# A fourth buffer for the experts' gate matrices, and expert code for twelve experts in a loop

## The reference

```python
# D_MODEL = 1024, 4 groups x 8 experts = 32, TOP_K = 2, D_EXPERT = 512
_, gsel = lax.top_k(lg, 1)                       # one of 4 groups for each token
tv, ti = lax.top_k(le_g, TOP_K)                  # two of its 8 experts
gates = jnp.sum(jax.nn.one_hot(eid, N_EXPERTS) * w[..., None], axis=1)
for e in range(N_EXPERTS):
    h = jax.nn.silu(x @ w_g[e]) * (x @ w_u[e])   # gate (1024x512) and up (1024x512)
    y = y + gates[:, e:e + 1] * (h @ w_d[e])     # down (512x1024)
return x + y                                     # then a final RMSNorm
```

## Time and profile before

| | us |
|---|---|
| three runs | 890.99, 897.95, 897.75; median 897.75 |
| profiled execution, device time | 895.14 |
| its span, first to last instruction | 892.7 |
| TensorE busy | 764.6 (86%) |
| mean share of the DMA engines' time, queue q1 | 69.6% |
| DMA traffic in all | 255.37 MB |

### The profile page before, as it was taken

One profiled execution on the slowest core, in us unless ns is written; L12 is line 12 of the kernel. 1 busy time (PEld: TensorE's weight loads), 2 busy tenths in 40 slices (PEclk: granted clock), 3 DMA queues, 4 the chain that ended last, 5 costly groups with the idle time before them and its releaser, 6 DMA issues.

```text
span 892.7 us, 15309 instructions
## 1 busy us (share of the span) xinstructions
PE 764.6 (86%) x5066; PEld 489.9 (55%) x5067; DVE 319.7 (36%) x754; ACT 214.0 (24%) x445; POOL 168.7 (19%) x380
## 2 busy tenths in 40 slices
PE   6999967799799982999979888879999999999740
PEld 3555545558454552666645454546666666666420
DVE  3578698850224334222212111112122212222117
ACT  4001235401331221122221122112222222222113
POOL 2015013200001002222222122112222222222100
PEclk9999988995889995899999899989999999999885
DMA  8202061171853349499999999999999949999965
GB/s 353 80 1 109 31 76 53 21 224 20 307 206 122 137 189 379 169 418 417 419 418 420 417 420 418 419 419 419 419 403 378 417 194 390 417 422 416 417 242 246
DMA packets 59593, 255.37 MB, mean 286 GB/s; under 512 B 19851, under 2 KB 22795, under 8 KB 36369
## 3 DMA queue, kind: packets, MB, share of 16 engines
q1 hardware_dynamic: 52560, 242.86, 69.6%
q0 software_dynamic: 6240, 11.46, 3.4%
q10 hardware_dynamic: 768, 0.72, 0.2%
HBM read 241.38 MB, written 22.30 MB: 295 GB/s over the span
## 4 chain that ended last, share of the span: by engine, by line
PE 57%; DMA 16%; SPq 13%; DVE 8%; ACT 3%; issue 2%; POOLq 0%; POOL 0%; DVEq 0%; ACTq 0%
PE pair L944 15%; PE pair L966 9%; DMA slot<-in_w_exp_up 7%; PE pair L742 7%; PE pair L605 6%; SPq L331 4%; SPq L334 4%; DMA reg_f<-in_w_exp_up 4%; SPq L325 3%; PE pair L945 3%; DMA slot<-in_w_in_qkv 2%; PE pair L847 2%; PE pair L920 2%; PE pair L606 2%; PE pair L667 2%
## 5 line engine op out<-in xcount | busy, mean ns | idle before, releaser
L944 PE MATMUL pair<-slot,probs 128*64 128x256 f32 x800 | 189.3, 398 | 22.8 <-DMA slot<-in_w_exp_up 21.7
L945 PE MATMUL pair<-slot,probs 128*64 128x256 f32 x800 | 189.5, 398 | 0.0
L944 PEld LDWEIGHTS pair<-slot,probs 128*64 128x64 f32 x800 | 114.3, 144 | 78.5 <-issue 46.3
L1590 DVE TENSOR_TENSOR sums<-iota_t,sums 128x640 bf16<-128x640 f32 x38 | 32.0, 841 | 259.0 <-POOL sums L536 252.9
L945 PEld LDWEIGHTS pair<-slot,probs 128*64 128x64 f32 x800 | 114.4, 144 | 0.0
L944 PE MATMUL pair<-reg_h,probs 128*64 128x256 f32 x384 | 88.1, 389 | 8.5 <-DMA reg_f<-in_w_exp_up 8.4
L966 PE MATMUL pair<-slot,sums 128*64 128x512 f32 x400 | 91.3, 597 | 4.5 <-ACT sums L1156 4.5
L945 PE MATMUL pair<-reg_f,probs 128*64 128x256 f32 x384 | 88.2, 389 | 0.0
L512 POOL DMA_INDIRECT probs<-hf_scr,row_u x38 | 40.1, 1056 | 240.4 <-DVE row_u L1602 183.8
L605 PE MATMUL pair<-reg_h,slot 128*128 128x512 f32 x160 | 82.4, 597 | 2.9 <-DVEq L1245 1.9
L1648 DVE TENSOR_TENSOR probs<-pair,probs 64x256 f32<-64x256 f32 x74 | 31.5, 426 | 136.9 <-ACT probs L1154 91.2
(11 more groups left out here) (365 smaller groups left out, 1033.1 us busy)
## 6 DMA issues: line engine op xcount, KB each, us to landing
slot<-in_w_exp_gate SPq DMA_DIRECT2D x22, 2048.0 KB, 22.8
slot<-in_w_exp_up SPq DMA_DIRECT2D x22, 2048.0 KB, 26.9
slot<-in_w_exp_down SPq DMA_DIRECT2D x44, 1024.0 KB, 24.0
reg_h<-in_w_exp_gate SPq DMA_DIRECT2D x10, 2048.0 KB, 23.9
reg_f<-in_w_exp_up SPq DMA_DIRECT2D x10, 2048.0 KB, 28.7
reg_h<-in_w_exp_down SPq DMA_DIRECT2D x10, 512.0 KB, 21.0
reg_f<-in_w_exp_down SPq DMA_DIRECT2D x10, 512.0 KB, 21.8
probs_t<-in_w_exp_down SPq DMA_DIRECT2D x10, 512.0 KB, 21.9
```

The source lines that it names most:

```text
L944: pe.matmul(gu[j][0:TT], lhs, gate_w[q][:, h, c, out], start=n == 0, stop=n == KD - 1)
L945: ins = pe.matmul(gu[j][TT:P], lhs, up_w[q][:, h, c, out], start=n == 0, stop=n == KD - 1)
L1590: tt(sel, iota_t[:].unsqueeze(1).to_broadcast([P, NT, P]), place_of[:, 0].unsqueeze(2).to_broadcast([P, NT, P]), ALU.is_equal)
```

## The change

Four buffers for gate matrices in place of three; the fourth is `reg_x`, columns 0 to 4095. Expert e now uses gate buffer e % 4 and, as before, up and down set e % 3. Expert 3's gate matrix is loaded ahead of the loop, behind the last load of expert 2, once the five tiles of normed rows are transposed (`xf_tr`) and stored (`hf_kept`). In the loop SyncE issues, for expert e: up(e), gate(e + 1), and after `y_ready` down(e). Gate(e + 1) goes where the gate matrix of expert e - 3 was, so it waits for the same event as up(e). The last expert has no gate matrix behind its up matrix.

Since 3 and 4 buffers come round together after twelve experts, TensorE's loop has twelve bodies and runs twice; experts 24 to 31 are written out behind it. SyncE's loop has twelve bodies from expert 3 on and runs twice, with experts 27 to 31 behind it.

```diff
@@ -202,7 +202,7 @@
 
 
         halves = lambda x: x.rearrange("p (h c n) -> p h c n", h=2, c=4)
-        gate_w = [halves(r[:, 0:4096]) for r in (slot[0], slot[1], reg_h)]
+        gate_w = [halves(r[:, 0:4096]) for r in (slot[0], slot[1], reg_h, reg_x)]
         up_w = [halves(r) for r in (slot[0][:, 4096:8192], slot[1][:, 4096:8192], reg_f[:, 0:4096])]
         down_w = [[x[:, 8192 + D * k:8192 + D * k + D] for k in range(KH)] for x in slot]
         down_w += [[reg_h[:, 4096:5120], reg_f[:, 4096:5120], probs_t[:], kv_f[:, 0:D]]]
@@ -244,10 +244,11 @@
             y_copied fin_out fin_sq fin_ms fin_sqrt fin_done sc_read base_step place_ready rows_done
             pow_ready ffn_ms ffn_sqrt fin_ss""".split()
 
-        names += [f"{n}_in{q}" for n in ("gate", "up", "down") for q in range(3)]
+        names += [f"{n}_in{q}" for n, held in (("gate", 4), ("up", 3), ("down", 3)) for q in range(held)]
         names += [f"got{i}" for i in range(NT)]
         s = {n: sem(n) for n in names}
-        gate_in, up_in, down_in = [[s[f"{n}_in{q}"] for q in range(3)] for n in ("gate", "up", "down")]
+        gate_in, up_in, down_in = [[s[f"{n}_in{q}"] for q in range(held)]
+                                   for n, held in (("gate", 4), ("up", 3), ("down", 3))]
         got_in = [s[f"got{i}"] for i in range(NT)]
 
         block = ctx.enter_context(nc.Block())
@@ -320,8 +321,10 @@
             sp.dma_start(o["state_prompt"], h_last[:]).then_inc(s["states_out"], 16)
             sp.dma_start(o["state_sample"], h_dec[:]).then_inc(s["states_out"], 16)
 
-            def load_gate_up(q, e):
-                sp.dma_start(gate_w[q], gate_v[e]).then_inc(gate_in[q], 16)
+            def load_gate(g, e):
+                sp.dma_start(gate_w[g], gate_v[e]).then_inc(gate_in[g], 16)
+
+            def load_up(q, e):
                 sp.dma_start(up_w[q], up_v[e]).then_inc(up_in[q], 16)
 
             def load_down(q, e):
@@ -335,7 +338,8 @@
 
 
             sp.wait_ge(s["y_ps"], 8)
-            load_gate_up(0, 0)
+            load_gate(0, 0)
+            load_up(0, 0)
             load_down(0, 0)
 
 
@@ -376,21 +380,28 @@
             sp.wait_ge(s["pairs_used"], 1)
             sp.dma_start(down_w[2][KH - 1], down_v[2, :, 1, 1]).then_inc(down_in[2], 16)
 
+            sp.wait_ge(s["xf_tr"], NT)
+            sp.wait_ge(s["hf_kept"], 16 * NT)
+            load_gate(3, 3)
+
             sp.wait_ge(s["pos_done"], 1)
 
-            def load_expert(q, e):
+            def load_expert(n, e, more):
 
                 done = sp.value_load(first_i[0:1, bass.ds(e - 2, 1)], min_val=1, max_val=TILES_MAX)
                 sp.wait_ge(s["gu_ready"], done)
-                load_gate_up(q, e)
+                load_up(n % 3, e)
+                if more:
+                    load_gate((n + 1) % 4, e + 1)
                 sp.wait_ge(s["y_ready"], done)
-                load_down(q, e)
-
-            with sp.Fori(1, NE // 3) as it:
-                for q in range(3):
-                    load_expert(q, it * 3 + q)
-            for e in range(NE - NE % 3, NE):
-                load_expert(e % 3, e)
+                load_down(n % 3, e)
+
+            rounds = (NE - 3) // 12
+            with sp.Fori(0, rounds) as it:
+                for n in range(12):
+                    load_expert(3 + n, it * 12 + (3 + n), True)
+            for e in range(3 + 12 * rounds, NE):
+                load_expert(e, e, e + 1 < NE)
 
             done = sp.value_load(first_i[0:1, NE - NE % 3:NE - NE % 3 + 1], min_val=1, max_val=TILES_MAX)
             sp.wait_ge(s["y_ready"], done)
@@ -929,19 +940,21 @@
             turn()
             pe.wait_ge(s["pos_done"], 1)
 
-            def expert(q, e, loads):
-
+            def expert(n, e, rounds):
+
+                g, q = n % 4, n % 3
+                gates, loads = rounds * 3 + (n // 4 + 1), rounds * 4 + (n // 3 + 1)
                 first, end = tiles_of(pe, e)
                 with pe.Fori(first, end) as w:
                     pe.wait_ge(s["xt_copied"], w + 1)
-                    pe.wait_ge(gate_in[q], loads * 16)
+                    pe.wait_ge(gate_in[g], gates * 16)
                     pe.wait_ge(up_in[q], loads * 16)
                     for j in range(2):
                         out = slice(256 * j, 256 * j + 256)
                         for n in range(KD):
                             h, c = n // 4, n % 4
                             lhs = xt_e[:, c, TT * h:TT * h + TT]
-                            pe.matmul(gu[j][0:TT], lhs, gate_w[q][:, h, c, out], start=n == 0, stop=n == KD - 1)
+                            pe.matmul(gu[j][0:TT], lhs, gate_w[g][:, h, c, out], start=n == 0, stop=n == KD - 1)
                             ins = pe.matmul(gu[j][TT:P], lhs, up_w[q][:, h, c, out], start=n == 0, stop=n == KD - 1)
                         ins.then_inc(s["gu_half" if j == 0 else "gu_ready"], 1)
 
@@ -968,11 +981,11 @@
                                             start=k == 0, stop=k == KH - 1)
                     ins.then_inc(s["y_ready"], 1)
 
-            with pe.Fori(0, NE // 3) as it:
-                for q in range(3):
-                    expert(q, it * 3 + q, it + 1)
-            for e in range(NE - NE % 3, NE):
-                expert(e % 3, e, NE // 3 + 1)
+            with pe.Fori(0, NE // 12) as it:
+                for n in range(12):
+                    expert(n, it * 12 + n, it)
+            for e in range(NE - NE % 12, NE):
+                expert(e % 12, e, NE // 12)
 
 
         @block.scalar
```

## The result

The changed kernel takes **890.45 us** (median of 20 runs, 887.96 to 897.61), the kernel before 897.13 (20 runs on the same chip); the ratio is 0.9943 with a 95% interval of 0.9926 to 0.9960. In three later sessions it was 0.9966 (0.9941 to 0.9990), 0.9936 (0.9910 to 0.9962) and 0.9933 (0.9899 to 0.9968). The forecast was 889.0. The profiled execution took 890.42 us with a span of 888.2.

What follows compares the result with a forecast made beforehand. Bound taken as the experts' weight stream, with TensorE the bound from 607 to 736 us. On the 892.7 us span: -9.0 + 2.0 = -7.0, so 885.7; as device time 888.1 or 890.7, given as 889.0; range 881.5 to 900.0.

Steps and rivals of the forecast that it cites:

- the case: Whole kernel: 9.0 us gained from the weight stream less 2.0 us for code, 885 to 891.5 us; chance 0.50.
- That rival: Ahead of the experts: expert 3's gate matrix delays the first gather by up to 5.4 us, 890 to 894; chance 0.10.
- the one of the unused buffer: Expert loop: SyncE comes too late for the fourth buffer, only the order changes, 895 to 898 us; chance 0.05.
- First stretch: Up to expert 17: up matrix lands 5.4 us earlier, down matrix does not, so 3.4 us gained.
- Last stretch: Restart to expert 31's up matrix: 19 matrices instead of 20 at 5.50 us each, 5.5 us gained.
- the prediction's meeting at expert 30: Expert 30's down product: TensorE free at 831.8 us, its down matrix there at 831.9.
- the term that was mis-sized: Code packets of the twelve-body loop: one more on the slowest DMA engine in each weight-bound stretch, +2.0 us.
- The slower rival: Weight-bound stretches: all code packets on one DMA engine, net +3 to +8 us, 898 to 905; chance 0.15.
- The jump back: TensorE between experts 11 and 12: a short stall is hidden in the 4.0 us an expert leaves free.
- the Trainium skill's rule: TensorE's loop: a taken branch outside the 2-page window forces a fetch; the prediction doubted this, given 128 KiB or 2048 instructions.
- No idle piece of 2 us or less should bring: Waits inside tiles ahead of down products: too short to bring half clock, 0.66 us a matmul in place of 0.40.
- The dent: Late in the expert loop: the dip in DMA activity becomes 6 us wide in place of 9.

Runs made afterwards that it cites:

- e12: The kernel before, unchanged, profiled and timed once more: ratio 0.9996.
- e1: The kernel before with only the twelve-body loops on TensorE and SyncE, three gate buffers and the old load order: ratio 1.0011.
- e2: The changed kernel with gate(e + 1) issued behind down(e) instead of ahead of it: ratio 0.9946.
- e6: The kernel before, old order, six bodies ahead of a three-body loop, fourth buffer for the gate matrices of experts 3 and 31 only: ratio 0.9972.
- e9: e10 plus four unused products ahead of TensorE's wait for expert 17 and four ahead of that for expert 30: 888.64 us, ratio 0.9895.
- e10: e6 with experts 15 to 17 written out, without unused products: 891.66 us, ratio 0.9938.
- e5: e2 with five unused products ahead of TensorE's wait for expert 31: ratio 0.9984.
- e11: The changed kernel as it is, run again against the kernel before: ratio 0.9933.
- e8: The changed kernel as it is, run again in another session against the kernel before: ratio 0.9936.
- e4: The kernel before with TensorE's loop at six bodies and two experts behind it, SyncE as before: ratio 0.9982.
- e7: e6 with the fourth buffer used for expert 3 alone, every later gate matrix loaded as before: ratio 0.9962.

## Why the prediction was right, and where it was off

**Direction and size.** Forecast 7.0 us on the profiled span, which became 4.5 us shorter; the expert part gave 4.4, and the timed median 6.7. The range and the case (a smaller stream, part of the gain given to code and to waits inside the tile) were right.

**Expert 3's gate matrix ahead of the loop.** Issued at 347.04 (forecast 346). It holds nothing up: the first gather takes 6.65 us (6.5 to 6.8 in the four profiles), for 7.18 in the earlier trace rows and 6.15 in e12. That rival fell, and so did the one of the unused buffer, since SyncE issues gate(e + 1) 0.6 us behind up(e).

**First stretch.** The mechanism was right: up(17) early, down(17) not, so the down product waits for the down matrix, at 614.42 (forecast 612.5 to 614). The gain is 1.5 us by the means of the table, in place of 3.4. Up(17) lands 3.4 us earlier for a forecast of 5.4. e1 attributes most of the difference to code: down(17) lands 1.1 to 1.5 us later by the code alone, and 0.1 to 0.5 us more in the changed kernel, which stay open. e2 shows the waiting itself to be the order's doing.

**Last stretch.** From restart to up(31) it takes 106.6 to 106.9 us, 3.5 less than before; forecast 5.5. e6, e9 and e10, without the twelve bodies, measure 105.0 to 105.2, so one matrix less is worth 5.1 and the changed kernel gives 1.4 to 1.9 of it back. e1 has 1.3 of code there; the rest may lie in the order of the loads, in which e6, e9 and e10 differ too. Nor did the prediction's meeting at expert 30 hold: it had TensorE free for that down product at 831.8 us and the matrix there at 831.9, without a wait. TensorE was free at 833.5, as late as the first stretch had made it, and the matrix landed at 835.7, 101.0 us behind the restart in place of 99.0:

```profile
835.89 6.42 PE L979 MATMUL pair<-slot,sums 128*64 128x512 f32 x16 [2.36 <-DMA slot<-in_w_exp_down]
```

**The code: the term that was mis-sized.** 39 packets came, within the 35 to 45 forecast, and I put 2.0 us on the sum for them. e1 gives 2.5 us, and it is up to 3.0 with the 1.4 to 1.9 of the last stretch in place of e1's 1.3. The count was right; one more on the slowest engine in each stretch, at 1.0 us, was too little. On which engines the packets fell no view shows. The slower rival, all packets on one engine, would have made the kernel 3 to 8 us slower and is excluded. The jump back cost a gap of 3.3 us without a releaser (in all four profiles; 5.0 and 4.9 in e2 and e5), inside the slack of the first stretch as the prediction had it: expert 17's tile is governed by the landing of its down matrix alone. On the Trainium skill's rule in "Runtime: NRT & Kernel Launch", section on instruction fetch mechanics: the packets disagree with its 2-page window (six bodies are jumped back over with no new load) and are compatible with its 2048 instructions for TensorE, which lie between six bodies and twelve: a tile shows 207 instructions of TensorE in the trace (its weight loads, waits and branches with it), and some 230 as I count them in the program.

**"No idle piece of 2 us or less should bring" the slow clock: this step failed.** Expert 30's down product, shown above, follows a wait of 2.36 us in a tile that had no wait ahead of it, and takes 6.42 us; in the first stretch of the same profile waits of 1.8 to 2.5 us are followed by down products of 5.1 to 5.4 us in six tiles, and waits of 1.7 to 2.3 us by products of 3.65 in three. Of its timeline two rows, and the stretches of these two products (the granted clock stands third from the end):

```profile
485.42 5.35 PE L979 MATMUL pair<-slot,sums 128*64 128x512 f32 x16 [2.10 <-DMA slot<-in_w_exp_down]
...
501.32 3.65 PE L979 MATMUL pair<-slot,sums 128*64 128x512 f32 x16 [1.68 <-DMA slot<-in_w_exp_down]
...
485.40:490.80 5.40, 5.35 (x16) 1.78 (x16) 0.00 (x0) 0.00 (x0) 0.39 (x3) 0.68 1.01 413
501.30:505.00 3.70, 3.65 (x16) 1.26 (x16) 0.00 (x0) 0.00 (x0) 0.81 (x4) 1.00 0.98 409
```

In e11 it came behind a still shorter one:

```profile
581.58 5.31 PE L979 MATMUL pair<-slot,sums 128*64 128x512 f32 x16 [1.20 <-DMA slot<-in_w_exp_down]
```

So it is not the wait's length alone that decides: after 2.52 us e8 ran expert 30's at full clock. The 1.5 to 1.7 us of each slow product of the first stretch lie in slack, and so do the 2.8 at expert 30 but for 0.5. So the false step cost the forecast little. On the other side, taking the long waits ahead of the tiles away, which is where the prediction saw a gain at expert 30 alone, was worth more than it said: where such a wait comes back at the end of a stretch (tile 17 in e2, e4, e6, e7, e10), 2.6 to 3.0 us are lost.

**The dent.** Forecast 6 us wide in place of 9, from the last landing at 727.0 to a restart 3.4 us earlier. The last landing ahead of it is that of the second half of down(24), at 704.27 + 24.8 = 729.07:

```profile
704.27 0.35 SPq L334 DMA_DIRECT2D slot<-in_w_exp_down  x1
...
slot<-in_w_exp_down SPq DMA_DIRECT2D x1, 1024.0 KB, 24.8
```

The next load is issued at 734.67, so the dent is 5.6 us wide (5.5 to 5.6 in the four profiles, 9.1 and 9.2 in the two of before). The width was forecast rightly, but for other dates, and that is luck: in the count of the table the restart came 1.5 us earlier and not 3.4, and the last landing 2.2 us later and not at the same time. The DMA engines do not run dry together; over the last 9.7 us ahead of the restart their share is already down to 0.19.

**The sum of the miss** in the expert part: forecast 7.0, that is 9.0 less 2.0 for code; measured 4.4. The first stretch gave 1.5 for its term of 3.4 (1.9 less), the last one 3.5 for 5.5 up to the landing of up(31) (2.0 less), and the slow product took 0.5: some 4.4 us short of the 9.0. Of them code is 2.5 to 3.0, of which 2.0 had been set aside; 0.4 is that a matrix is worth 5.1 and not 5.5; 0.5 the slow product; and 0.5 to 1.0 is open. That the median came out close to 889.0 all the same (6.7 us less, where the expert part gives 4.4) is luck: no run shows where the other 2.3 us come from, and the part ahead of the experts varies by more than that.

## What to carry to other kernels

Where a stream of loads is the bound, moving one load ahead moves only the landings of what stands in front of it; look which operand of the last tile then lands last, and reorder with that tile in mind. The tile that ends a bound stretch hands its own length on: a wait of 4 us ahead of it costs 2 to 3 us more by the clock, and a few unused products in the wait bring them back, while a wait in the tiles between lies in slack. When the whole program varies by more than the effect, count from an event inside it: here 485 us repeated within 0.6 while the 360 ahead of them moved by 7.

## What the runs showed of the hardware

- The granted clock can fall behind a wait of 1.2 to 2.5 us inside a tile (down product 5.0 to 6.6 us for 3.65; 0.68 granted for 1.00), and it need not (3.65 after 2.52 us, e8).
- The time that TensorE needs behind a wait of some 4 us varies, from 7.1 us at full clock (one tile of e4) to 10.1 (tile 17 of e6), for the same products.
- A loop of three or six bodies is loaded once (16 and 19 packets of code in the run), one of twelve again on its second pass (39 or 40, with one gap of 3.3 to 5.0 us at the jump back). Beside a saturated stream of weights the 24 additional packets of e1 cost 2.5 us, about 0.1 us each.
